# Final norm of a decoder trunk: scale and weight row applied after the transposes, sums of squares in two pieces

## The reference

```python
def rmsnorm(x, g):
    xf = x.astype(jnp.float32)
    y = xf * lax.rsqrt(jnp.mean(xf * xf, axis=-1, keepdims=True) + EPS)
    return (y * g.astype(jnp.float32)).astype(x.dtype)
...
    y = rmsnorm(x, norm_final)
```

## Time and profile before

| | |
|---|---|
| median of three runs | 2544.62 us (2541.22 to 2547.41) |
| the profiled execution | 2543.95 us, of which its span is 2542.1 us |
| mean granted clock of TensorE | 0.971 of 2.4 GHz |
| TensorE busy | 2348.9 us, 92% of the span |
| VectorE, ScalarE, POOL busy | 1313.8, 604.4, 664.6 us |
| final norm and stores | from 2506.60 us to the end of the span |

### The profile page before, as it was taken

One profiled execution on the slowest core, in us unless ns is written; L12 is line 12 of the kernel. 1 busy time (PEld: TensorE's weight loads), 2 busy tenths in 40 slices (PEclk: granted clock), 3 DMA queues, 4 the chain that ended last, 5 costly groups with the idle time before them and its releaser, 6 DMA issues. The chain is left out here.

```text
span 2542.1 us, 37838 instructions
## 1 busy us (share of the span) xinstructions
PE 2348.9 (92%) x15139; PEld 2225.0 (88%) x15139; DVE 1313.8 (52%) x2106; ACT 604.4 (24%) x966; POOL 664.6 (26%) x588
## 2 busy tenths in 40 slices
PE   5989999999999988999799999999999997989996
PEld 5879999999999987898689799879979985978985
DVE  4463444323231354555747764774687476535555
ACT  2431111000000023222322321330232033332223
POOL 0012233232323322222113422332342332321220
PEclk9989999999999999999889999999999998999998
DMA  4663232222222224444222423332332332244432
GB/s 143 197 192 112 93 102 87 83 92 96 93 92 91 91 83 142 148 153 158 80 86 84 118 79 106 108 92 87 94 113 87 114 97 70 97 154 148 158 113 97
DMA packets 288351, 281.55 MB, mean 111 GB/s; under 512 B 10666, under 2 KB 251980, under 8 KB 287151
## 3 DMA queue, kind: packets, MB, share of 16 engines
q1 hardware_dynamic: 197592, 124.87, 16.8%
q0 software_dynamic: 24912, 85.47, 9.3%
q10 hardware_dynamic: 65711, 69.32, 8.4%
HBM read 173.48 MB, written 23.73 MB: 78 GB/s over the span
## 5 line engine op out<-in xcount | busy, mean ns | idle before, releaser
L822 PE MATMUL acc<-h_hi,w_hi 128*128 128x344 f32 x2232 | 491.7, 329 | 31.0 <-POOL w_lo L681 16.8
L681 POOL TENSOR_TENSOR w_lo<-w_raw,w_hi 128x1024 fp32r<-128x1024 f32 x153 | 389.8, 2548 | 432.5 <-DMA w_hi<-w_raw 432.5
L822 PE MATMUL acc<-h_lo,w_hi 128*128 128x344 f32 x2232 | 477.0, 322 | 0.0
L822 PE MATMUL acc<-h_hi,w_lo 128*128 128x344 f32 x2232 | 474.6, 321 | 0.0
L822 PEld LDWEIGHTS acc<-h_hi,w_hi 128*128 128x128 f32 x2232 | 378.4, 190 | 43.4 <-issue 24.9
L822 PEld LDWEIGHTS acc<-h_lo,w_hi 128*128 128x128 f32 x2232 | 380.8, 191 | 0.0
L822 PEld LDWEIGHTS acc<-h_hi,w_lo 128*128 128x128 f32 x2232 | 375.8, 189 | 0.0
L677 POOL TENSOR_TENSOR zero<-zero 128x1 f32<-128x1 f32 x173 | 44.7, 258 | 1146.2 <-issue 682.6
L1978 DVE TENSOR_TENSOR x<-acc,x 128x1032 f32<-128x1032 f32 x96 | 118.2, 1232 | 255.7 <-PE acc L847 255.7
L1021 PE MATMUL acc<-y_hi,w_hi 128*128 128x344 f32 x384 | 129.1, 336 | 11.6 <-DVE x L2163 7.3
L1021 PE MATMUL acc<-y_hi,w_lo 128*128 128x344 f32 x384 | 124.3, 324 | 0.0
(11 more groups left out here) (309 smaller groups left out, 4234.1 us busy)
## 6 DMA issues: line engine op xcount, KB each, us to landing
w_hi<-w_raw POOLq DMA_DIRECT2D x153, 512.0 KB, 2.9
w_raw<-in_w_in_even SPq DMA_DIRECT2D x48, 512.0 KB, 3.7
w_raw<-in_w_in_odd SPq DMA_DIRECT2D x41, 512.0 KB, 3.7
cache<-in_cache_mem_k ACTq DMA_DIRECT2D x8, 2048.0 KB, 8.5
cache<-in_cache_mem_v ACTq DMA_DIRECT2D x8, 2048.0 KB, 8.1
w_raw<-in_w_xa_k SPq DMA_DIRECT2D x16, 512.0 KB, 4.3
w_raw<-in_w_xa_v SPq DMA_DIRECT2D x16, 512.0 KB, 4.0
w_raw<-in_w_out_even SPq DMA_DIRECT2D x16, 512.0 KB, 3.7
```

Source lines behind the costliest of these rows:

```text
L681: pool.tensor_tensor(lo, raw_ap, hi.bitcast(F32), ALU.subtract).then_inc(done, 1)
L822: ins = pe.matmul(acc[a][:, n * 512:n * 512 + CH], wt[:, s, w], mv[:, k, n * CH:(n + 1) * CH], start=(k == 0 and j == 0), stop=(k == KT - ...
```

## The change

Scale and weight are applied after the transposes, when tokens are rows: `x` is transposed as it is, and VectorE makes each tile of `y_out` out of the accumulator in one operation, with `rstd` as a scalar per partition and the weight as a row that is the same on all partitions. ScalarE's copies, the spreading of the scales and the scaling of `x` go. The weight row is loaded by SP into `w_raw[1]`, 4 KB to each partition, once the last unit of slot 1 is split. The token sums come in two pieces: five tiles as soon as two thirds are added (`FIRST` = 2 * 344 // 128 = 5), and the rest behind the transposes of tile 2; the roots and reciprocals follow in two pieces too. In `scale_tiles` the branches for the final norm go; what it does for the earlier norms stays.

```diff
+        FIRST = 2 * CH // P
+
+        GAIN_AT = 1
...
             cross(1)
 
+            assert t.turn == GAIN_AT
+            sp.wait_ge(w_split[GAIN_AT], t.slot[GAIN_AT])
+            sp.dma_start(w_raw[:, GAIN_AT, :], ins["norm_final"].rearrange("(a d) -> a d", a=1).partition_broadcast(P)
+                         .rearrange("p a d -> p (a d)")).then_inc(tables, 16)
             for i in range(TT + 1):
                 rows = P if i < TT else NB
                 sp.wait_ge(y_ready, i + 1)
...
             cross(1, 4, [(s_keep, 11, 8 * i) for i in range(3)])
 
-            norm(5)
+            def late_sums(tiles):
+
+                for i in tiles:
+                    rows = P if i < TT else NB
+                    ins = pe.matmul(M0[0:rows, i:i + 1], sum_late[:, i * P:i * P + rows], one, start=True, stop=True)
+                ins.then_inc(summed, 1)
+
+            pe.wait_ge(sq_added, added_at[5] + 14)
+            late_sums(range(FIRST))
+            for b in range(NCH):
+                pe.wait_ge(job_out[b], jobs[0] // NCH)
             for i in range(TT + 1):
                 rows = P if i < TT else NB
                 if i < 2:
                     a = begin(i % 2 ^ 1)
-                    pe.wait_ge(fin_ready, KT)
                 else:
                     a, _, _ = t.next(i % 2 ^ 1)
                     pe.wait_ge(y_ready, i - 1)
                 for k in range(KT):
                     ins = pe.transpose(acc[a][0:rows, k * P:(k + 1) * P], x[:, k, i * P:i * P + rows], ident)
                 ins.then_inc(result, 1)
+                if i == 2:
+                    pe.wait_ge(sq_added, added_at[5] + 21)
+                    late_sums(range(FIRST, TT + 1))
...
             cross(1, 4, PRM_XA + KT, waits, conv_rows)
-            norm(5)
-            for i in range(TT + 1):
-                a, r, _ = t.next(i % 2 ^ 1)
-                rows = P if i < TT else NB
-                act.wait_ge(result, r)
-                if i >= 4:
-                    act.wait_ge(y_stored[i % 4], 16 * (i // 4))
-                act.activation(y_out[0:rows, i % 4, :], acc[a][0:rows, 0:D], ACT.Copy).then_inc(y_ready, 1)
+            act.wait_ge(summed, scales_at(5))
+            act.activation(sd[:, 0:FIRST], M0[:, 0:FIRST], ACT.Sqrt, bias=eps, scale=1.0 / D).then_inc(root_ready, 1)
+            act.wait_ge(summed, scales_at(5) + 1)
+            act.activation(sd[:, FIRST:TT], M0[:, FIRST:TT], ACT.Sqrt, bias=eps, scale=1.0 / D).then_inc(root_ready, 1)
+            act.activation(sd[0:NB, TT:TT + 1], M0[0:NB, TT:TT + 1], ACT.Sqrt, bias=eps[0:NB], scale=1.0 / D).then_inc(root_ready, 1)
...
             cross(1, 4, PRM_XA + KT)
-            norm(5, PRM_FIN)
+            gain = w_raw[:, GAIN_AT, :]
+            dve.wait_ge(tables, 16 * 10)
+            for i in range(TT + 1):
+                rows = P if i < TT else NB
+                a, r, _ = t.next(i % 2 ^ 1)
+                if i in (0, FIRST):
+                    tiles = slice(0, FIRST) if i == 0 else slice(FIRST, TT + 1)
+                    dve.wait_ge(root_ready, 2 * scales_at(5) - (1 if i == 0 else -1))
+                    dve.reciprocal(rstd[:, tiles], sd[:, tiles]).then_inc(rstd_ready, 1)
+                    dve.wait_ge(rstd_ready, scales_at(5) + (0 if i == 0 else 1))
+                dve.wait_ge(result, r)
+                if i >= 4:
+                    dve.wait_ge(y_stored[i % 4], 16 * (i // 4))
+                dve.scalar_tensor_tensor(out=y_out[0:rows, i % 4, :], in0=acc[a][0:rows, 0:D], scalar=rstd[0:rows, i:i + 1],
+                                         in1=gain[0:rows, :], op0=ALU.mult, op1=ALU.mult).then_inc(y_ready, 1)
```

More of the change, by code:

```diff
@@ L402, in build @@
         exped = sem("exped")
-        fin_ready = sem("fin_ready")
         g_ready = sem("g_ready")
@@ L1998, in scale_tiles @@
             def scale_tiles(n_th, gain, scale_bc):
-                split = n_th < 5
                 for j in range(KT):
-                    if split and j >= 2:
+                    if j >= 2:
                         dve.wait_ge(lo_ready, 8 * (n_th - 1) + j - 1)
[L2004 to L2014, removed]
+                    dve.scalar_tensor_tensor(out=h32[:, j % 2, :], in0=x[:, j, :], scalar=prm_col(gain + j), in1=scale_bc[:, :],
+                                             op0=ALU.mult, op1=ALU.mult).then_inc(h32_ready, 1)
+                    if j:
+                        lo_half(n_th, j - 1)
+                lo_half(n_th, KT - 1)
+                dve.wait_ge(lo_ready, 8 * n_th)
             def lo_half(n_th, j):
```

## The result

The changed kernel takes 2519.90 us (median of four runs, 2517.32 to 2521.14). The kernel before, run beside it, takes 2546.01 (four runs, 2541.22 to 2549.81); the first three of those are the runs that the prediction had. The ratio is 0.9897, 95% interval 0.9877 to 0.9917: faster by 26 us where 19.2 were forecast. The profiled execution took 2521.14 us.

What follows compares the result with a forecast made beforehand. TensorE bounds most of the span, but a chain of waits decides the last 36 us. Gains of 15.38, 1.51, 1.71 and 0.6 made 19.2; 2543.95 less that, plus 0.67 to the median, gave 2525.4 us, range 2521 to 2531.5.

Steps and rivals of the forecast that it cites:

- Spreading and scaling: Between rstd and the first transpose: spreading, ScalarE's copy and eight scalings of x leave the chain, 15.38 us less.
- Sums and roots: From last addition of squares to first VectorE operation: 1.30 us instead of 2.81, 1.51 less; 0 without the early sums.
- First tile: First finished tile: VectorE's operation of 1.29 us replaces transposes and ScalarE's copy of 3.00, 1.71 us less.
- From first tile to end: From first finished tile to the span's end: 13.7 us instead of 14.3, 0.6 less, with VectorE's pitch of 1.25 as bound.
- the stall ahead of the fourth tile: Among the final tiles: VectorE waits 0.7 us because TensorE makes the second piece of sums behind tile 2.
- Weight row: SP's 512 KB load during the last head's attention: costs nothing, landing some 50 us before it is wanted.
- Ahead of the last addition: Everything before the last addition of squares ends at 2506.60: untouched by the change, so no gain was counted there.
- the prediction's own sign of being wrong: Stated failure test: anything ahead of 2500 us in the changed profile shifted by more than the scatter.
- Half clock: Rival, chance 0.25: TensorE falls to 1.2 GHz among the final transposes, costing 1.6 to 3.1 us; time 2527 to 2528.5.
- The ring of four: Rival, chance 0.07: every final store takes 5.4 us, so tiles wait for stores at 1.67 us each; time 2527.8.
- The split does nothing: Rival, chance 0.04: first piece of sums not ahead of the last additions, roots 1.4 us later, no stall; time 2526.1.
- Slower VectorE: Rival, chance 0.04: VectorE's nine final operations on PSUM run longer than 1.25 us, making the kernel slower or the same.

Runs made afterwards that it cites:

- a4: Changed kernel with the token sums of all nine tiles in one piece after the last addition, roots and reciprocal made once: 2527.63 us (one run).
- b4: Changed kernel with VectorE's operation made twice for each tile, first into a buffer nobody reads: 2531.11 us (one run).
- a3: Kernel before with only the weight row's load and its two waits added, the row not read: 2546.51 us, ratio 1.0010 to the kernel before.
- c1: a4 with tile 0's transposes put ahead of the one-piece sums, to fill TensorE's wait: 2523.54 us (one run).
- b2: Changed kernel with the dropped semaphore `fin_ready` put back unused, restoring the old semaphore numbers: 2518.47 us, ratio 0.9905 to the kernel before.

## Why the prediction was right, and where it was wrong

**Spreading and scaling, 15.38.** Right: no row of either is left after 2500, and what they took went from the chain.

**Sums and roots, 1.51.** Right. First VectorE operation 1.35 us after the last addition (2505.28 - 2503.93), forecast 1.30, behind the table load as said. a4 shows that the sentence behind the term, that without the early sums 1.51 would be lost, was too narrow: 3.7 were, since the transposes then wait behind the sums as well and run at 1.2 GHz.

**First tile, 1.71.** Right: the operation takes 1.28, and the first tile is ready 2.6 after the last addition.

**From first tile to end, 0.6.** Mis-sized: it was 1.6. It took 2519.3 - 2506.57 = 12.7, where 13.7 stood. The tiles came 0.45 sooner, counted from start to start: 0.2 by a pitch of 1.22 for 1.25, and 0.2 because the stall ahead of the fourth tile added 0.5 to a pitch and not 0.7 (VectorE's idle time there is 0.43); the second reciprocal added the 0.2 forecast. The other 0.5 is the end: 2.8 us were put behind the last operation (a store of 2.2 and 0.6 for what follows), and from 2516.99 to 2519.3 it is 2.3. For the pitch, the prediction set the duration of one operation against an estimate of 1.19 from the Trainium skill (VectorE: DVE Perf Modes, The TRN2 errata). That mixed two things: 1.28 is one operation's duration, and the pitch at which they follow each other is 1.22 on average, in b4 1.19 to 1.20. The estimate is close to the pitch that the traces show.

**Weight row, 0.** Right as far as the traces show: it is issued 56 us early, and a3 gains nothing by it.

**Ahead of the last addition, 0, and the range.** These are the steps that failed. The sum puts nothing on the head, and the prediction's own sign of being wrong was a shift there by more than the scatter. By the split near 228 us the changed kernel's profiles are 3.1 us ahead on average, each of them ahead of the profiles without the change in its group; how much of that is left at the end, whole runs put at 1.6 with a standard error of 0.9 (21.8 less 20.1), and what causes it stays open. The low end of the range then took -3.4 from the scatter of three runs and 0.9 from the terms, with nothing for how well the base or a median of four is known. The 62 runs of before have a mean of 2543.4, 1.2 below the median that the forecast started from; the first four runs of after lie 1.7 below the mean of its 15 (2519.9 against 2521.6). So the 5.5 us between 2525.4 and 2519.9 are, rounded, 1.2 and 1.7 from small samples, 0.9 from the tail (20.1 for 19.2), and 1.6 that the tail doesn't account for. The first two are luck, and all four went one way.

**Rivals.** *Half clock* didn't decide the result but is real: one of four profiles of this order of work, at 1.3 us there (16.7 against 15.4), near its lower price of 1.6. *The ring of four* is out: all stores land in 2.6 to 2.7. *The split does nothing* is out by the rows of the first piece. *Slower VectorE* is out: nine operations of 1262 to 1284 ns.

## What to carry to other kernels

A chain of single-engine steps at the end of a kernel can be priced from its rows, step by step, to within 1 us of 20; what the steps overlap with afterwards (here: whether the transposes fill TensorE's wait) can be worth more than the step that is moved. Take the pitch of operations back to back, not one's duration, where an engine is the bound. Size the range from how well the base itself is known: three runs of a 2.5 ms kernel don't tell 3 us. And compare a landmark far ahead of the edit in every profile of both kernels: an edit at the end came with a beginning that was 3 us quicker, which looked like drift in one pair of profiles.

## What the runs showed of the hardware

TensorE's clock fell behind one-column matmuls, in a4 (0.50 from 2508 on), c1 and b2 while the engine read as fully busy, and in the kernel before near 2508.7. One-column matmuls aren't needed for it: in b4 it fell at 2520.3 among transposes alone, behind a wait of 1.50, while a wait of 1.51 among transposes left it at 1.00 in after. Stores of 512 KB at one per 1.2 us land in 2.6 us each with the DMA engines full (share 1.02, 418 GB/s); the 409 GB/s of before, from which 1.28 a tile was reckoned, was not the ceiling. And 62 runs of the kernel before lie 16 us apart (2535.44 to 2551.39), with two of its profiles 2.1 us apart by 230 us into the span.
